# Opening experts' gather matrices from ranks inside the compacted set, slot arithmetic behind the opening product, low parts on GpSimd, and no unread products

## What is computed

```
def hier_moe(h, w_rg, b_rg, w_re, b_re, w_g, w_u, w_d):   # t: 384 x 1024
    lg = t @ w_rg + b_rg                                  # 4 groups
    oh_g = one_hot(argmax(lg), 4)
    p_sel = sum(softmax(lg) * oh_g)
    le = (t @ w_re + b_re).reshape(-1, 4, 8)              # 8 experts in each group
    top_v, top_i = top_k(einsum('tge,tg->te', le, oh_g), 2)
    wk = softmax(top_v) * p_sel
    comb = oh_g[:, :, None] * sum(one_hot(top_i, 8) * wk[..., None])[:, None, :]
    for g in range(4):
        a = einsum('td,edf->tef', t, w_g[g]); u = einsum('td,edf->tef', t, w_u[g])
        out += einsum('tef,efd->td', silu(a) * u * comb[:, g, :, None], w_d[g])
```

## Time and profile before

| | us |
|---|---|
| median of 3 runs | 645.97 |
| lowest and highest | 645.27, 647.68 |
| the profiled execution's own time | 646.17 |
| its span, first to last instruction | 644.4 |

### The profile page before, as it was taken

One profiled execution on the slowest core, in us unless ns is written; L12 is line 12 of the kernel. 1 busy time (PEld: TensorE's weight loads), 2 busy tenths in 40 slices (PEclk: granted clock), 3 DMA queues, 4 the chain that ended last, 5 costly groups with the idle time before them and its releaser, 6 DMA issues.

```text
span 644.4 us, 9476 instructions
## 1 busy us (share of the span) xinstructions
PE 630.5 (98%) x3529; PEld 425.9 (66%) x3529; DVE 337.5 (52%) x730; ACT 255.6 (40%) x490; POOL 126.9 (20%) x142
## 2 busy tenths in 40 slices
PE   9999999999999999999999999999999999999995
PEld 7878888877888777778777888764434434343431
DVE  5555347894546665754356763666333524334312
ACT  6583343336524556655934334431211311221200
POOL 0018426663001311010000100022201401210311
PEclk9999999999999999999999999999999999999999
DMA  8975432353323844205977998489999999999992
GB/s 349 412 293 178 150 130 99 118 213 131 109 85 115 286 139 150 74 34 159 337 247 284 427 378 327 166 325 365 426 426 423 428 427 426 424 429 425 426 419 113
DMA packets 35152, 175.09 MB, mean 272 GB/s; under 512 B 4208, under 2 KB 4480, under 8 KB 22688
## 3 DMA queue, kind: packets, MB, share of 16 engines
q1 hardware_dynamic: 32128, 163.30, 64.9%
q0 software_dynamic: 2976, 11.16, 4.9%
HBM read 167.48 MB, written 7.48 MB: 272 GB/s over the span
## 4 chain that ended last, share of the span: by engine, by line
PE 79%; DMA 7%; SPq 7%; ACT 2%; DVE 2%; issue 1%; POOL 0%; POOLq 0%; DVEq 0%; ACTq 0%
PE banks L1758 15%; PE banks L1760 15%; PE banks L1759 15%; PE banks L2158 11%; SPq L857 7%; PE banks L2188 6%; DMA piece<-in_wexp 4%; DMA raw<-in_wstream 3%; PE banks L2142 2%; PE banks L1983 1%; PE banks L2198 1%; ACT w_hi_lo L1049 1%; PE banks L2063 1%; DVE w_hi_lo L1292 1%; PE banks L1950 1%
## 5 line engine op out<-in xcount | busy, mean ns | idle before, releaser
L1292 DVE TENSOR_TENSOR w_hi_lo<-raw,w_hi_lo 128x1024 fp32r<-128x1024 f32 (+1 forms) x82 | 120.4, 1478 | 79.2 <-ACT w_hi_lo L1049 77.4
L1758 PE MATMUL banks<-w_hi_lo,hT_hi 128*128 128x512 f32 x312 | 124.6, 399 | 0.8 <-DVE w_hi_lo L1292 0.4
L1760 PE MATMUL banks<-w_hi_lo,hT_lo 128*128 128x512 f32 x312 | 121.7, 390 | 0.0
L1759 PE MATMUL banks<-w_hi_lo,hT_hi 128*128 128x512 f32 x312 | 121.6, 390 | 0.0
L1049 ACT ACTIVATE w_hi_lo<-raw 128x1024 fp32r<-128x1024 f32 x78 | 82.3, 1057 | 89.0 <-PE banks L1760 81.3
L2158 PE MATMUL banks<-piece,xs 128*64 128x512 f32 x512 | 114.7, 593 | 0.6 <-DMA piece<-in_wexp 0.6
L2158 PEld LDWEIGHTS banks<-piece,xs 128*64 128x64 f32 x512 | 38.7, 137 | 72.6 <-issue 68.9
L1758 PEld LDWEIGHTS banks<-w_hi_lo,hT_hi 128*128 128x128 f32 x312 | 58.6, 188 | 13.3 <-issue 1.9
L1760 PEld LDWEIGHTS banks<-w_hi_lo,hT_lo 128*128 128x128 f32 x312 | 58.6, 188 | 12.6
L1759 PEld LDWEIGHTS banks<-w_hi_lo,hT_hi 128*128 128x128 f32 x312 | 58.7, 188 | 11.2
L2188 PE MATMUL banks<-piece,act_T 128*64 128x512 f32 x256 | 58.5, 598 | 0.1
(11 more groups left out here) (367 smaller groups left out, 951.0 us busy)
## 6 DMA issues: line engine op xcount, KB each, us to landing
piece<-in_wexp SPq DMA_DIRECT2D x90, 1024.0 KB, 18.9
raw<-in_wstream SPq DMA_DIRECT2D x80, 512.0 KB, 4.3
piece<-in_wexp SPq DMA_DIRECT2D x12, 512.0 KB, 17.9
foxc<-in_foxc POOLq DMA_DIRECT2D x8, 512.0 KB, 5.1
memv<-in_memc SPq DMA_DIRECT2D x8, 512.0 KB, 5.7
memk<-in_memc SPq DMA_DIRECT2D x8, 512.0 KB, 5.7
xT<-in_xT SPq DMA_DIRECT2D x1, 1536.0 KB, 7.0
xtok<-in_xtok SPq DMA_DIRECT2D x1, 1536.0 KB, 11.5
```

The source lines that it names most:

```text
L1292: dve.tensor_tensor(w_lo[:, i % PART_SLOTS, cols], raw[:, i % RAW_SLOTS, cols], w_hi[:, i % PART_SLOTS, cols].bitcast(F32), ALU.subtract). ...
L1758: mm(out, xh, wh, start=start, stop=False, skip_group_check=True)
L1759: mm(out, xh, wl, start=False, stop=False, skip_group_check=True)
L1760: return mm(out, xl, wh, start=False, stop=stop, skip_group_check=True)
```

## The change

- `r_first`, the place of a token in group 0's set, is taken from the group ranks by one product with the group's one-hot; the rest of what `route_group` did behind the ranks moves to `route_sets`, in the step `slots`. The table `before` now includes the diagonal, so ranks count from 1.
- The slots of the first four experts no longer come through the expert ranks, `route_slots` and `info` 1. `opening_rows` multiplies `pick_group` with `opening_taken` (which of the four experts each token chose), ACT copies the result as bf16 (`opening_b`), `opening_ranks` ranks it inside the compacted set by one product, DVE multiplies the two, and `pick_half` compares with the slot number.
- The slot arithmetic, with the member matrices and the inputs of the exponentials, moves behind the opening's first product `gu` 0.
- The low part of half 1 is made by POOL from SBUF; the twelve PE instructions of `second_whole` and `second_low`, the three copies on ACT and `neg_ident` are gone. The second compaction takes tiles 0 and 1 first and tile 2 in the step `compact_rest`.
- The eleven unread products are gone.
- The order of the opening steps is another, and the four halves of the gather use banks 5, 3, 5, 3.

The schedule:

```diff
     step("compact", 0, 0, 0)
     step("compact", 0, 1, 1)
+    plain("opening_rows", 0)
+    s.append(("compact_rest", 0, 1, 1, None))
+    s.append(("compact_low", 0, 0, 0, None))
+    plain("opening_ranks", 0)
+    plain("ranks", 0)
+    plain("pick_half", 0, 0)
+    step("gather_half", 0, 0, 5)
+    step("gu", 0, 0, 2)
+    s.append(("compact_low", 0, 1, 1, None))
+    plain("pick_half", 0, 1)
     plain("slots", 0)
-    s.append(("compact_low", 0, 0, 0, None))
+    step("gather_half", 0, 1, 3)
+    step("gather_half", 1, 0, 5)
     plain("info", 1)
-    plain("pick_half", 0, 0)
-    s.append(("compact_low", 0, 1, 1, None))
-    for j in range(2):
-        step("gather_half", 0, j, 5 + j)
-    plain("pick_half", 0, 1)
     plain("weights", 0)
+    step("gather_half", 1, 1, 3)
+    plain("info", 2)
+    step("rows", 0, 0, 7)
     for p in range(PAIRS):
...
-        step("gu", p, 0, 2 + p % 2)
-        if p == 0:
-            plain("info", 2)
-            for j in range(2):
-                step("gather_half", 1, j, 5 + j)
-            step("rows", 0, 0, 7)
+        if p:
+            step("gu", p, 0, 2 + p % 2)
```

DVE's part, cut to its core:

```diff
             dve.wait_ge(rank_ready, 1)
-            rank = ps[:, 6, T * NR:T * NR + 4 * T].rearrange("p (t n) -> p t n", t=T)
+            chain(dve.tensor_tensor(r_first, group_ranks()[:, :, 0], v(r_oh, 4)[:, :, 0], ALU.mult))
...
+        def route_sets(dve, chain):
+
             pos, mine = v(r_t4, 4), v(r_d4, 4)
-            dve.tensor_tensor(pos, rank, v(cst2("first_slot"), 36)[:, :, 32:36], ALU.add)
-            chain(dve.scalar_tensor_tensor(mine, rank, float(P), v(r_oh, 4), ALU.is_lt, ALU.mult))
+            dve.wait_ge(rank_ready, 2)
+            dve.tensor_tensor(pos, group_ranks(), v(cst2("first_slot"), 36)[:, :, 32:36], ALU.add)
+            chain(dve.scalar_tensor_tensor(mine, group_ranks(), float(P + 1), v(r_oh, 4), ALU.is_lt, ALU.mult))
             chain(dve.tensor_tensor(pos, pos, mine, ALU.mult))
             chain(dve.tensor_reduce(r_slots.rearrange("p (t r) -> p t r", t=T)[:, :, 2], pos, AX, ALU.add))
...
+            chain(dve.tensor_tensor(r_both, r_oh1, r_oh2, ALU.add))
+            dve.tensor_tensor(opening_taken[:, :, :], v(r_both, 8)[:, :, 0:4], v(r_oh, 4)[:, :, 0:1].to_broadcast([P, T, 4]), ALU.mult).then_inc(opening_step, 1)
+            dve.tensor_tensor(v(taken_b[:, :], NR)[:, :, 0:32].rearrange("p t (g e) -> p t g e", g=NG), v(r_oh, 4).unsqueeze(3).to_broadcast([P, T, NG, NE]),
+                              v(r_both, 8).unsqueeze(2).to_broadcast([P, T, NG, NE]), ALU.mult).then_inc(taken_ready, 1)
...
                 elif what == "slots":
+                    route_sets(dve, chain)
                     route_slots(dve, chain)
...
                 elif what == "pick_half":
-                    dve.wait_ge(info_out, 2)
-                    cols = slice(P * j, P * j + P)
-                    chain(dve.tensor_scalar(pick[:, cols], cst2("iota1")[:, cols], r_mine[:, 0:1], None, ALU.is_equal))
-                    dve.scalar_tensor_tensor(pick[:, cols], cst2("iota1")[:, cols], r_mine[:, 1:2], pick[:, cols].bitcast(F32), ALU.is_equal, ALU.add).then_inc(pick_ready, 1)
+                    if j == 0:
+                        dve.wait_ge(opening_step, 4)
+                        chain(dve.tensor_tensor(r_opening, ps[:, 4, 280:284], opening_b[:, :], ALU.mult))
+                    dve.tensor_tensor(pick[:, P * j:P * j + P].rearrange("p (e s) -> p e s", e=2), cst2("iota1")[:, 0:CAP].unsqueeze(1).to_broadcast([P, 2, CAP]),
+                                      r_opening[:, 2 * j:2 * j + 2].unsqueeze(2).to_broadcast([P, 2, CAP]), ALU.is_equal).then_inc(pick_ready, 1)
```

ACT, POOL and PE:

```diff
-                    if i == 1:
-                        for t in range(T):
-                            act.wait_ge(xlo_psum, t + 1)
-                            act.activation(x_lo[i][t][:, :], ps[:, t, :], ACT.Copy).then_inc(xparts_ready, 1)
...
+                elif what == "opening_rows":
+                    act.wait_ge(opening_step, 2)
+                    act.activation(opening_b[:, :], ps[:, 4, 272:276], ACT.Copy).then_inc(opening_step, 1)
...
+            def second_low(t):
+
+                pool.wait_ge(xhi_ready, T + t + 1)
+                pool.tensor_tensor(x_lo[1][t][:, :], x2[:, t, 512:1024], x_hi[1][t][:, :].bitcast(F32), ALU.subtract).then_inc(xlo_second, 1)
...
+                elif kind == "x_parts" and i == 1:
+                    second_low(0)
                 elif kind == "route":
...
+                    second_low(1)
+                    second_low(2)
...
+                elif what == "opening_rows":
+                    pe.wait_ge(opening_step, 1)
+                    for t in range(T):
+                        ins = mm(ps[:, 4, 272:276], pick_g[:, t, :], opening_taken[:, t, :], start=t == 0, stop=t == 2, **kw)
+                    ins.then_inc(opening_step, 1)
+                elif what == "compact_rest":
+                    pe.wait_ge(xlo_second, T)
+                    mm(ps[:, b0, :], pick_g[:, T - 1, :], x_hi[j][T - 1][:, :], start=False, stop=False, **kw)
+                    mm(ps[:, b0, :], pick_g[:, T - 1, :], x_lo[j][T - 1][:, :], start=False, stop=True, **kw).then_inc(compact_done, 1)
+                elif what == "opening_ranks":
+                    pe.wait_ge(opening_step, 3)
+                    mm(ps[:, 4, 280:284], before_b[:, :], opening_b[:, :], start=True, stop=True, **kw).then_inc(opening_step, 1)
...
-                    if a == 1:
-                        unread_passes(5)
-                elif what == "slots":
+                elif what == "ranks":
                     token_ranks(1, 0, 32, [NR * t for t in range(T)])
-                    unread_passes(6)
```

More of the change, by code:

```diff
@@ L508, in program @@
         info_parts = at("info_parts", [P, T, 6, 2], o_ot + 12 * KB + 512 + 4 * NRT + 32, F32R)
+        opening_taken = at("opening_taken", [P, T, 4], o_z + 111 * KB, F32R)
         assert 12 * KB + 512 + 4 * NRT + 32 + 48 * T <= 18 * KB
@@ L734, in program @@
         r_rows = R(2 * NG).bitcast(I32)
+        r_first, r_opening, r_both = R(T), R(4), r_t8
         r_lost_f = R(T)
@@ L792, in route_slots @@
             chain(dve.tensor_tensor(pos, rank, v(cst2("first_slot"), NR)[:, :, 0:32], ALU.add))
-            chain(dve.scalar_tensor_tensor(pos, rank, float(CAP), pos, ALU.is_lt, ALU.mult))
+            chain(dve.scalar_tensor_tensor(pos, rank, float(CAP + 1), pos, ALU.is_lt, ALU.mult))
             x3 = r_x[:, 0:64 * T].rearrange("p (t r e) -> p t r e", t=T, r=2)
@@ L1204, in _ @@
                     act.activation(r_e2, r_d2, ACT.Exp).then_inc(route_exp, 1)
-                elif what == "compact":
+                elif what == "opening_rows":
+                    act.wait_ge(opening_step, 2)
+                    act.activation(opening_b[:, :], ps[:, 4, 272:276], ACT.Copy).then_inc(opening_step, 1)
+                elif what == "compact" and j == 0 or what == "compact_rest":
                     act.wait_ge(compact_done, j + 1)
@@ L1444, in _ @@
                 if what == "pick_group" and a == 0:
[L1445 removed]
                     for t in range(T):
[L1447 removed]
+                        ins = dve.tensor_scalar(pick_g[:, t, :], cst2("iota1")[:, 0:P], r_first[:, t:t + 1], None, ALU.is_equal)
                     ins.then_inc(pick_group, 1)
@@ L2065, in _ @@
                         ins.then_inc(x2t_lg_ready, 1)
-                elif kind == "x_parts" and i == 1:
-                    second_whole(0)
-                    second_low(0)
                 elif kind == "route":
-                    second_whole(1)
                     token_ranks(0, 32, 4, [T * NR + 4 * t for t in range(T)])
-                    second_low(1)
-                    second_whole(2)
-                    second_low(2)
-            kw = dict(skip_group_check=True)
-            def unread_passes(n):
-                for _ in range(n):
-                    mm(ps[:, 2, :], pick_g[:, 0, :], x_hi[0][0][:, :], start=True, stop=True, **kw)
             def bank_free(old):
@@ L2102, in _ @@
                     pe.wait_ge(pick_group, 1)
-                    pe.wait_ge(xparts_ready, 2 * T if j else T + 1)
-                    for t in range(T):
+                    pe.wait_ge(xparts_ready, T)
+                    for t in range(T - j):
+                        if j:
+                            pe.wait_ge(xlo_second, t + 1)
                         for x in (x_hi, x_lo):
                             ins = mm(ps[:, b0, :], pick_g[:, t, :], x[j][t][:, :], start=t == 0 and x is x_hi, stop=t == 2 and x is x_lo, **kw)
-                    ins.then_inc(compact_done, 1)
+                    if j == 0:
+                        ins.then_inc(compact_done, 1)
+                elif what == "opening_rows":
[10 more added lines that the diff above has]
+                    mm(ps[:, 4, 280:284], before_b[:, :], opening_b[:, :], start=True, stop=True, **kw).then_inc(opening_step, 1)
                 elif what == "info":
@@ L2279, in constants @@
```

(4 more changed lines are left out.)

30 lines of the change are left out of this document (12 added, 18 removed).

## The result

The changed kernel takes 655.53 us (median of 4 runs, 653.81 to 657.9) against 645.74 for the kernel before (4 runs): a ratio of 1.0146, 95% interval [1.0126, 1.0166]. The medians differ by 9.8 us, 1.5%. The profiled execution took 656.15 with a span of 654.3 and a mean granted clock of 0.982. The forecast was 647.4 within 645.0 to 651.0.

What follows compares the result with a forecast made beforehand. The end was set by when the transfers become continuous, PE's bound being close. `gu` 0 came 3.1 earlier but `gu_rest` 0 1.4 later: span 644.4 + 1.4, plus 1.8 around it, less 0.2 for the median: 647.4, range 645.0 to 651.0.

Steps and rivals of the forecast that it cites:

- They are hidden: Second compaction: POOL's low parts, 1.29 per operation, end about 415.1, tile 2 is wanted at 418.1, so they cost nothing.
- POOL is slow: Rival: half 1's low parts take twice as long on POOL, 0.6 us more, 648.0; chance 0.04.
- Worth nothing: Routing: the removed low-part PE instructions and three ACT copies had nothing waiting behind them, so removal gains nothing.
- return nothing: Opening: the eleven removed unread products lay in DVE's shadow, so removing them changes no time.
- the clock falls in the opening: Rival: PE, nearly empty from 411.5 to 415.1, drops to half clock, slowing compaction and first gather; 650.4, chance 0.26.
- the second rival: Clock falls ahead of `gu_rest` 0 as PE stands from 428.2 to 431.5; 2.5 us more, 649.9, chance 0.12.
- The prediction's working: Behind `gu` 0: list order ties PE to ACT and DVE, so `gu_rest` 0 starts at 432.1, 1.4 later than before.
- the two stands: Behind `gu` 0: PE stands over 1 us before `info` 2 and again before the turned `rows`.
- The rival without a hold behind `gu` 0: Exponentials come before `gather_half` 1 0, `gu_rest` 0 starts 1.8 earlier, transfers limit the gain: 644.5, chance 0.08.

Runs made afterwards that it cites:

- a: Changed kernel with the low parts of half 1 made on PE and copied out by ACT again: 650.77 us, +4.6 over the kernel before.
- b: Changed kernel plus unread products on PE in the routing, eighteen ahead of the group ranks and four behind; POOL keeps the low parts: 654.34 us.
- g: Changed kernel with each of POOL's 128x512 subtractions cut into four of 128x128: 654.80 us, +8.5 over the kernel before.
- j: Changed kernel with POOL copying x2 into half 1's x_lo instead of subtracting, so that low part is left out: 652.77 us, single run.
- d: Kernel before without its eleven unread products, nothing else changed: 648.82 us, +2.7.
- i: a with eleven unread products in PE's stands, six behind `gather_half` 1 1 and five behind `info` 2: 647.67 us, +1.7 over the kernel before.
- e: a with exponentials and weights ahead of the gather halves and `info` 1 bringing only its two slot columns: 644.33 us, -2.0 over the kernel before.
- f: Changed kernel with the list order of e alone, POOL keeping the low parts: 651.70 us, +5.4 over the kernel before.

## Why the prediction was wrong

**The step that failed: "They are hidden".** The low parts on POOL were costed by their own length against the time at which they are wanted, and that part was right (1.24 to 1.27 each, done at 415.04). Left out was what they do to DVE beside them. Three operations of the routing's chain stand until POOL's instruction ends, 2.9 us, and the chain is what everything waits for. c has the low parts on POOL and nothing else of the change (+5.0), a undoes them (-5.2), b shows `gu` 0 2.8 later by the hold alone, and g and j show that the hold is as long as POOL's instruction has left. The prediction came near it in "POOL is slow" (chance 0.04), but took it as POOL's own length doubled, 0.6 us at most. The Trainium skill has the rule in full on another page than the one cited: "SBUF — State Buffer", section "SBUF: two separate sides", says that VectorE and GpSimd share a pair of ports by an exclusive lock, that a VectorE operation with two inputs from SBUF and a GpSimd operation that reads SBUF both need it, and that whichever starts first has it for its whole instruction while the other waits. The rows agree: 1.19 for an operation of 12 columns with two inputs beside POOL, 0.17 for a reduce with one input, 0.38 beside the short pieces.

**"Worth nothing" and "return nothing".** The PE work removed had no reader that waited, but it kept PE from standing. The products of the low part lay where PE otherwise has only the nine small ranks; the eleven unread products lay in two stands behind the compaction. d prices the latter at 2.7 us in the kernel before, with nothing else changed; this is no price for the changed kernel, whose stands lie elsewhere. b's trace shows the clock at 1.00 through the routing once products lie there again. No run takes the low part off PE without a hold on DVE: the shortest stand seen ahead of the ranks is 2.80 (j), and the clock fell there too. The rival "the clock falls in the opening" named the mechanism and its price (650.4); it came together with the hold on DVE, which lengthened the stand of PE to 4.81, and with the second rival, the fall ahead of `gu_rest` 0.

**Behind `gu` 0.** The prediction's working held: the two stands are 1.40 and 1.04, the exponentials come behind five groups of ACT's copies, the first gather in a starts at 419.35 for 419.46 forecast, a's `gu_rest` 0 at 432.42 for 432.1, and with the stands filled (i) the loss is 1.7 for 1.4 forecast. (`opening_rows` has 0.33 in one place of the prediction and 0.47 in another; in a it takes 0.25, and nothing hangs on it.) What was given a chance of 0.12 is here the usual case: in the profiles of the changed kernel, of a, b, g and j, all that have this order and unfilled stands, the clock falls ahead of `gu_rest` 0. Filling the stands takes back 2.9 of a's 4.6 (the rival: 2.5).

**The other side.** The rival without a hold behind `gu` 0 said 644.5, a gain of 1.5, since the transfers have only 1.3 and 0.15 us to give. e, made to have none, takes 644.33 and gains 2.0 over the kernel before on its chip. `gu` 0 starts 3.0 earlier against `logits` than before and `gu_rest` 0 1.5 earlier. So here too the end follows `gu_rest` 0 and not `gu` 0. In every trace the transfers are at a share of 1.00 or 1.01 from 450 to 620 us, which fits; that it is they that allow no more is argued and not tested.

**The sum as measured.** Of the 9.8 us, 5.2 go with POOL's part (after less a): the hold on DVE and the low clock that comes with it. Of the other 4.6, 2.9 go when the stands behind `gu` 0 are filled (a less i), and 1.7 stay with the hold behind `gu` 0 (i). Of the 2.9, a's profile shows some 1.4: 0.97 in `gu_rest` 0 and 0.46 in `rows` (1.04 from its start to that of `gu_rest` 0, where i has 0.58). The rest lies in executions of a without a trace. The parts don't add freely: in the other order, POOL's part costs 7.4 (f less e).

**Still open.** Why the clock falls at 425.6 in the changed kernel, at 426.7 in f and at 421.1 in i's profiled execution isn't settled. All three lie at the end of the stand of 0.71 or 0.72 us ahead of `gu` 0, and a, b, e, g and j have the same stand and kept 1.00 there. In the changed kernel PE had stood only 0.28 and 0.71 us since `info` 0. There and in f the clock had only just come back from the low level (at 422.2 and 423.3); in i it had not been low, and a, whose steps up to that point are i's, kept 1.00. No run tells what makes the difference.

## What to carry to other kernels

Before elementwise work goes to GpSimd, look at what VectorE does in the same time: in the routing of these runs every small operation with two operands from SBUF stood until GpSimd's instruction ended, and in a chain of dependent ones each such stand adds to the chain. Work on TensorE that nobody waits for is not free to remove where it fills a stand: look at the granted clock over the products behind it. Filling a stand with products that nobody reads is the second choice (i, 647.67); the first is an order of the lists that leaves no stand (e, 644.33). A step moved behind a product is worth reading once more in the list order of every engine: here the same steps in another order turned +4.6 us into -2.0.

## What the runs showed of the hardware

- A DVE operation of 12 columns with two operands from SBUF took 1.05 to 1.19 us beside a 1.24 us subtraction on POOL, 0.24 and 0.38 beside pieces of 0.42, 0.39 and 0.52 beside a copy of 0.6, and 0.17 alone. A reduce with one operand took 0.17 beside any of them. A TENSOR_SCALAR of 128 columns with one tensor and a column of scalars took up to 0.49 beside the pieces and 0.28 alone.
- POOL's copy of 128x512 from SBUF took 0.59 to 0.62, its subtraction 1.24 to 1.27.
- TensorE's clock fell from 2.4 to 1.2 GHz ahead of the group ranks while PE stood 4.81 us, and stayed at the lower level from 411.9 to 422.2, through the compaction; `gu_rest` 0 took 3.65 us at the upper level and 5.67 for the most part at the lower.
- How long the clock is low is not the same in every execution of one kernel: a's four have a mean granted clock of 0.989 to 0.994 and take 648.73 to 652.03. e's six, with no stand behind `gu` 0, have 0.997 to 0.998 and take 644.18 to 644.81.
